# Rotary partner rows: fp32 permutation products on TensorE replaced by SBUF-to-SBUF transfers

## What is computed

```python
def apply_rope(x, cos, sin):           # first stack
    x1, x2 = jnp.split(x, 2, axis=-1)
    return jnp.concatenate([x1 * c - x2 * s, x2 * c + x1 * s], axis=-1)

def rotate(x, ang):                    # second stack, on each half of a head
    x1, x2 = x[..., :m], x[..., m:]
    return jnp.concatenate([x1 * cos - x2 * sin, x2 * cos + x1 * sin], axis=-1)
```

## Time and profile before

| | us |
|---|---|
| median of 3 runs | 2303.76 |
| lowest, highest run | 2297.82, 2307.5 |
| span of the profiled execution | 2301.2 |
| PE busy in it | 2258.3 (98%) |
| DVE busy | 1462.8 (64%) |
| ACT busy | 847.0 (37%) |
| POOL busy | 160.2 (7%) |

### The profile page before, as it was taken

The page is one execution under the profiler, slowest core; times in us unless marked ns, Lnnn a source line. Parts: engine busy times, 40 slices in busy tenths (PEclk is TensorE's granted clock), DMA queues, the critical chain, the costliest instruction groups (busy, mean ns, idle before and its releaser), DMA issues.

```text
span 2301.2 us, 37388 instructions
## 1 busy us (share of the span) xinstructions
PE 2258.3 (98%) x14172; PEld 2033.1 (88%) x14172; DVE 1462.8 (64%) x2310; ACT 847.0 (37%) x1130; POOL 160.2 (7%) x235
## 2 busy tenths in 40 slices
PE   8999999999999999999999999999999999999998
PEld 8999999999999988888888888888888888879998
DVE  4547777556778787678778767773333346556555
ACT  4445444435634432222432222232212234445443
POOL 0110000130000110001001101000000001000000
PEclk9999999999999999999999999999999999999999
DMA  6225665323665565455335545433233223123553
GB/s 230 98 74 195 206 239 174 124 83 103 210 237 187 180 207 183 164 192 177 106 130 204 182 162 199 160 115 110 77 105 109 71 95 127 56 74 128 173 192 128
DMA packets 65483, 343.21 MB, mean 149 GB/s; under 512 B 7152, under 2 KB 10480, under 8 KB 42608
## 3 DMA queue, kind: packets, MB, share of 16 engines
q1 hardware_dynamic: 44656, 266.47, 33.3%
q0 software_dynamic: 20736, 75.51, 9.8%
HBM read 340.90 MB, written 1.05 MB: 149 GB/s over the span
## 4 chain that ended last, share of the span: by engine, by line
PE 79%; issue 11%; DVE 6%; ACT 3%; DMA 1%; POOL 0%; DVEq 0%; SPq 0%; ACTq 0%; POOLq 0%
PE gpt L841 20%; PE gpt L843 19%; PE gpt L842 19%; DVE w_lo L1951 2%; ACT w_hi L1461 2%; PE gpt L938 1%; PE gpt L766 1%; PE gpt L939 1%; PE gpt L940 1%; PE gpt L767 1%; PE gpt L768 1%; PE mbt L1121 1%; PE gpt L1336 1%; PE gpt L1337 1%; PE gpt L1338 1%
## 5 line engine op out<-in xcount | busy, mean ns | idle before, releaser
L841 PE MATMUL gpt<-xn_hi,w_hi 128*128 128x512 f32 (+2 forms) x2256 | 747.3, 331 | 5.7 <-DVE w_lo L1951 5.7
L842 PE MATMUL gpt<-xn_lo,w_hi 128*128 128x512 f32 (+2 forms) x2256 | 742.8, 329 | 0.0
L843 PE MATMUL gpt<-xn_hi,w_lo 128*128 128x512 f32 (+2 forms) x2256 | 742.7, 329 | 0.0
L1951 DVE TENSOR_TENSOR w_lo<-raw,w_hi 128x2048 fp32r<-128x2048 f32 (+2 forms) x280 | 567.6, 2027 | 249.7 <-ACT w_hi L1461 249.5
L1461 ACT ACTIVATE w_hi<-raw 128x2048 fp32r<-128x2048 f32 (+2 forms) x280 | 476.4, 1702 | 390.9 <-PE gpt L843 356.5
L841 PEld LDWEIGHTS gpt<-xn_hi,w_hi 128*128 128x128 f32 x2256 | 426.5, 189 | 46.6 <-issue 7.1
L842 PEld LDWEIGHTS gpt<-xn_lo,w_hi 128*128 128x128 f32 x2256 | 426.6, 189 | 37.6
L843 PEld LDWEIGHTS gpt<-xn_hi,w_lo 128*128 128x128 f32 x2256 | 426.5, 189 | 37.5
L841 PE MATMUL gpt<-mid_hi,w_hi 128*128 128x512 f32 (+2 forms) x996 | 333.1, 334 | 4.7 <-DVE mid_lo L2149 4.5
L842 PE MATMUL gpt<-mid_lo,w_hi 128*128 128x512 f32 (+2 forms) x996 | 332.2, 334 | 0.0
L843 PE MATMUL gpt<-mid_hi,w_lo 128*128 128x512 f32 (+2 forms) x996 | 332.2, 334 | 0.0
(11 more groups left out here) (341 smaller groups left out, 2734.5 us busy)
## 6 DMA issues: line engine op xcount, KB each, us to landing
raw<-in_up_a SPq DMA_DIRECT2D x72, 1024.0 KB, 4.7
ada_w<-in_ada POOLq DMA_DIRECT2D x144, 512.0 KB, 3.5
raw<-in_up_b SPq DMA_DIRECT2D x60, 1024.0 KB, 4.8
raw<-in_down_a SPq DMA_DIRECT2D x48, 768.0 KB, 4.3
raw<-in_down_b SPq DMA_DIRECT2D x48, 640.0 KB, 3.9
raw<-in_win SPq DMA_DIRECT2D x16, 1024.0 KB, 4.8
raw<-in_qkv SPq DMA_DIRECT2D x12, 1024.0 KB, 4.8
raw<-in_wout SPq DMA_DIRECT2D x8, 1024.0 KB, 4.8
```

The costliest lines, as they stand in the source:

```text
L841: mm(o, w_hi[b][:, j, :], hi(k), start=(k == 0), stop=False)
L842: mm(o, w_hi[b][:, j, :], lo(k), start=False, stop=False)
L843: last = mm(o, w_lo[b][:, j, :], hi(k), start=False, stop=(k == kt - 1))
L1951: V.tensor_tensor(w_lo[b][:, 0:tiles, :], raw[b][:, 0:tiles, :], w_hi[b][:, 0:tiles, :].bitcast(F32), ALU.subtract).then_inc(lo_ready, 1)
```

## The change

The three permutation matrices leave `tab`, and the sine table gets the sign: minus in the rows whose partner lies above. The matrix products and their semaphore waits leave PE. In their place the partner rows are copied within SBUF by DMA, two tiles per transfer: for distance d, one DMA for each block of d partitions (2 for d = 64, 4 for 32, 8 for 16). DVE then multiplies the arrived rows by the sine in place, with both operands in SBUF, and adds as before.

```diff
+        def swap_parts(half):
+            return [(a, a ^ half) for a in range(0, P, half)]
 # SP, layer1: between the weight loads
-                for b in range(2):
-                    load(pl + 6, b, dram["rg"][L, 1 + b], MIX_TILES[4 + b])
+                sp.wait_ge(kpe_ready, L + 1)
+                sp.wait_ge(rope_done, L * ROPES1 + 8)
+                for a, c in swap_parts(ROPE // 2):
+                    sp.dma_start(swapped1(8)[a:a + ROPE // 2, :], kpe[c:c + ROPE // 2, :]).then_inc(swap_in[0], 16)
+                load(pl + 6, 0, dram["rg"][L, 1], MIX_TILES[4])
+                sp.wait_ge(qr_gain, L * 2 + 2)
+                sp.wait_ge(rope_done, L * ROPES1 + 9)
+                for a, c in swap_parts(ROPE // 2):
+                    sp.dma_start(ksq[a:a + ROPE // 2, 2:4, :], qf[c:c + ROPE // 2, 4:6, :]).then_inc(swap_in[1], 16)
+                load(pl + 6, 1, dram["rg"][L, 2], MIX_TILES[5])
 # PE: perm, its calls and its waits
-                mm(bank[:, 0:n], tab[:, cp:cp + P], tile, start=True, stop=True).then_inc(perm_ready, 1)
...
 # ACT, layer1
+                def swap(s):
+                    z, m = zq if s < S_RK else zk, 2 * (s % 2)
+                    act.wait_ge(evac_done, done_at(base + s))
+                    if s >= S_RK:
+                        act.wait_ge(rope_done, L * ROPES1 + 2 * (s - S_RK) + 2)
+                    for a, c in swap_parts(P // 2):
+                        nc.scalar.dma_start(ksq[a:a + P // 2, m:m + 2, :], z[c:c + P // 2, m:m + 2, :]).then_inc(swap_in[s % 2], 16)
...
                         copies(s0 + j, [z[:, 2 * j, :], z[:, 2 * j + 1, :]])
+                        if z is not zv:
+                            swap(s0 + j)
 # ACT, differential attention
+            def swap2(i):
+                s = rope2_slot(2 * i)
+                z, m = dq if i < 4 else dk, 2 * (i % 4)
+                act.wait_ge(evac_done, done_at(s))
+                if i >= 4:
+                    act.wait_ge(rope_done, DEPTH * ROPES1 + (4 if i == 4 else 6 if i == 5 else 8 if i == 6 else 10))
+                to = sqb[:, i % 4 if i < 4 else 1 + (i - 4) % 3, :].rearrange("p (h n) -> p h n", n=SEQ)
+                for a, c in swap_parts(16):
+                    nc.scalar.dma_start(to[a:a + 16, :, :], z[c:c + 16, m:m + 2, 0:SEQ]).then_inc(swap2_in[i % 4], 16)
...
                 q_evac(s)
                 split((S_QKV + s) // 2 + 1, s % 2, SIDE_T)
+                swap2(s)
...
             k_evac(0)
+            swap2(4)
             split(k_slot(1) // 2, 0, SIDE_T)
...
                         k_evac((u + 2) // 4)
+                        swap2(4 + (u + 2) // 4)
 # DVE, rope
-                dve.wait_ge(perm_ready, r0 + k + 1)
-                V.tensor_tensor(rb[:, k % 2, :], bank[:, 0:n], tab[:, cs:cs + n], ALU.mult).then_inc(rot_s, 1)
+                arrived(dve)
+                V.tensor_tensor(rb, rb, tab[:, cs:cs + n], ALU.mult).then_inc(rot_s, 1)
```

More of the change, by code:

```diff
@@ L99, in constant_tables @@
     t[64:, C_SEL1] = 1.0
[L101 to L111, removed]
     i = np.arange(P)
@@ L120, in rope @@
         t[:, cc:cc + pos.shape[-1]] = np.cos(ang)
-        t[:, cs:cs + pos.shape[-1]] = np.sin(ang)
+        t[:, cs:cs + pos.shape[-1]] = np.where((i % dim < half)[:, None], -np.sin(ang), np.sin(ang))
     tok = np.arange(T1)[None, :]
@@ L268, in build @@
         kpe_ready = sem("kpe_ready")
-        perm_ready, rot_c, rot_s, rope_done = sem("perm_ready"), sem("rot_c"), sem("rot_s"), sem("rope_done")
+        swap_in, swap2_in = [sem("swap_in0"), sem("swap_in1")], [sem(f"swap2_in{i}") for i in range(4)]
+        rot_c, rot_s, rope_done = sem("rot_c"), sem("rot_s"), sem("rope_done")
         vt_ready, v_ready = sem("vt_ready"), sem("v_ready")
@@ L425, in rope1 @@
             if k < 8:
-                return (zq if k < 4 else zk)[:, k % 4, :], C_PR, C_CR, C_SR
+                return (zq if k < 4 else zk)[:, k % 4, :], C_CR, C_SR
             if k == 8:
-                return kpe[:, :], C_PM, C_CM, C_SM
-            return qf[:, 4 + k - 9, :], C_PM, C_CM, C_SM
+                return kpe[:, :], C_CM, C_SM
+            return qf[:, 4 + k - 9, :], C_CM, C_SM
         def rope2(k):
-            return (dq if k < DHEADS else dk)[:, k % DHEADS, 0:SEQ], C_PD, C_CD, C_SD
+            return (dq if k < DHEADS else dk)[:, k % DHEADS, 0:SEQ], C_CD, C_SD
         DUNITS = [(h, q) for h in range(DHEADS) for q in range(2)]
@@ L450, in rope2_slot, with swapped1, swapped2, wait_swap @@
             return S_QKV + k // 2 if k < DHEADS else k_slot((k - DHEADS) // 2)
-        def rope2_bank(k):
-            return mb[1 + k % 2] if k < DHEADS + 2 else gp[0][k % 2]
+        def swapped1(k):
+            return ksq[:, k % 4 if k < 8 else 3 if k == 10 else 2, :]
+        def swapped2(k):
+            i = k // 2
+            side = sqb[:, i % 4 if i < 4 else 1 + (i - 4) % 3, :]
+            return side[:, (k % 2) * SEQ:(k % 2 + 1) * SEQ]
+        def swap_parts(half):
+            return [(a, a ^ half) for a in range(0, P, half)]
+        SWAPS1 = [2] * 4 + [4, 4]
+        def wait_swap(e, L, k):
+            n = k // 2 if k < 8 else 4 if k == 8 else 5
+            e.wait_ge(swap_in[n % 2], 16 * (L * sum(SWAPS1[n % 2::2]) + sum(SWAPS1[n % 2:n + 1:2])))
+        def wait_swap2(e, k):
+            i = k // 2
+            e.wait_ge(swap2_in[i % 4], 16 * (P // 16) * (i // 4 + 1))
         def wo_bank(m):
@@ L2294, in gated_residual, with rope @@
                 return go
-            def rope(r0, k, item, n, ra, rb, bank):
-                tile, _, _, cs = item
-                dve.wait_ge(perm_ready, r0 + k + 1)
-                V.tensor_tensor(rb[:, k % 2, :], bank[:, 0:n], tab[:, cs:cs + n], ALU.mult).then_inc(rot_s, 1)
+            def rope(r0, k, item, n, ra, rb, arrived):
+                tile, _, cs = item
+                arrived(dve)
+                V.tensor_tensor(rb, rb, tab[:, cs:cs + n], ALU.mult).then_inc(rot_s, 1)
                 dve.wait_ge(rot_s, r0 + k + 1)
                 dve.wait_ge(rot_c, r0 + k + 1)
-                V.tensor_tensor(tile, ra[:, k % 2, :], rb[:, k % 2, :], ALU.add).then_inc(rope_done, 1)
+                V.tensor_tensor(tile, ra[:, k % 2, :], rb, ALU.add).then_inc(rope_done, 1)
             def layer1(L):
@@ L2386, in layer1 @@
                 mix_split(2)
-                rope(L * ROPES1, 8, rope1(8), T1, rot_a, rot_b, ROT2[0])
+                rope(L * ROPES1, 8, rope1(8), T1, rot_a, swapped1(8), lambda e: wait_swap(e, L, 8))
                 q_squares(2)
@@ L2399, in layer1 @@
                 for k in (9, 10):
-                    rope(L * ROPES1, k, rope1(k), T1, rot_a, rot_b, ROT2[k % 2])
+                    rope(L * ROPES1, k, rope1(k), T1, rot_a, swapped1(k), lambda e, k=k: wait_swap(e, L, k))
                 k_squares(2)
@@ L2713, in d_rotations @@
                 for k in ks:
-                    rope(r0, k, rope2(k), SEQ, drot_a, drot_b, rope2_bank(k))
+                    rope(r0, k, rope2(k), SEQ, drot_a, swapped2(k), lambda e, k=k: wait_swap2(e, k))
             dve.wait_ge(xc_ready, ctx_tiles(9))
```

40 lines of the change are left out of this document (7 added, 33 removed).

## The result

The changed kernel takes 2323.0 us (median of 4 runs, 2317.0 to 2324.0) where the kernel before, timed once more beside it, takes 2304.8: a ratio of 1.0081, 95% interval 1.0062 to 1.0100. It is slower by 0.8%, 18 us, where the forecast was 7 us faster, and the time lies outside the range of 2288 to 2310. The profiled execution has a span of 2322.3 us against 2301.2. Timed again in a later session beside the kernel before, the same file gave 2321.1 (2313.1 to 2324.0), ratio 1.0067 (1.0045 to 1.0089).

The account below looks back on a forecast made before the run. The prediction took PE as the bound. Gains of 3.0 us in the two layers, 2.5 ahead of `d_scores(0)` and 1.2 in three units sum to 6.7, taking the median from 2303.8 to 2297.1, range 2288 to 2310.

Parts of the forecast that it names:

- The price of an issue: ACT's DMA issues: 0.39 us from one to the next, 0.34 for the last; two DMAs 0.73, eight 3.07.
- The clock: PE's granted clock: a half-clock stretch of 4 us costs 2; one more or less worth a few us, unassigned.
- I cost them at nothing: Differential attention, issues behind the `dq` copies: no cost, or about 1 us if ACT doesn't issue while it computes.
- What leaves PE: Permutation products removed from both layers and the differential attention: 18.6 us of PE time, if nothing else became late.
- First stack: Each layer: ACT waits for the rope, copies queue behind, PE waits 3.5 us before `k_pe`; 0.2 of 3.7 gained.
- `kpe`: Each layer's `kpe` transfers, issued by SP: last lands at 86.3, DVE wants it at 86.96, so no wait.
- `d_scores(0)`: Start of the differential attention's scores: PE waits 3.5 us for the key rope; gain 2.5 of 6.0 us.
- Units 2, 6, 10: Differential attention: `d_pv` released by `d_at`, gaining 0.4 of 0.86 us each, 1.2 us for three units.
- DVE: DVE's sine product, now reading SBUF twice: as many instructions as before, no cost for product and add together.
- Rival 2: ACT's queue becomes the bound: gain gone at 0.56 us per issue, 2307 to 2308 at 0.62; chance 0.15.
- Rival 1: Issues on ACT cost nearly nothing: gain 14.1 us, time 2289.7; chance 0.20.
- Rival 3: Transfers land late, after 6 us instead of 2.8: 8 us of the gain gone, 2305; chance 0.08.

## Why the prediction was wrong

**The forecast's span was 2294.5; it became 2322.3.** The gap of 27.8 us has three parts; the second and third are estimates.

- **The price of an issue, 11.7 us.** The step that failed is "I choose 0.39, the same kind of queue". The steps measured are 0.64 in the second stack (0.50 in the pairs of the first). From the first issue of a group to ACT's next instruction: in a layer 1.51 and 1.16 where 0.73 stood twice, 2.4 for both layers; 5.95 ahead of the split for `d_scores(0)` and 5.20 in each unit where 3.07 stood, 2.9 + 3 x 2.1. The earlier trace rows held both prices, and the reason given, the same kind of queue, holds for 0.62 as well as for 0.39: it chose nothing, and the upper end was the right one. SP itself shows that the queue was not what decides: it issues the `kpe` transfers in 0.6 each and, 6 us on, a weight load in 0.33:

```profile
83.49 2.50 SPq L528 DMA_DIRECT2D ksq<-kpe  x4
89.63 0.33 SPq L487 DMA_DIRECT2D raw<-in_rg  x1
```

- **The clock, about 12 us** (14 missing, of which 2 passed while PE stood). The prediction called it a term that it couldn't assign, "one more or less is worth a few us either way". But it forecast two new waits of PE of 3.5 us, in three places, and a wait has one sign: with the waits filled the clock never fell at these places. Leaving the term at zero was as large an error as the price.
- **The rest, 4 us.** "I cost them at nothing" was said of the `dq` issues. PE waits 1.4 us for splits and 0.5 for the norm between 1905 and 1970 us, 0.6 before the change: 1.3 us. It is what the prediction gave as the price if ACT couldn't issue beside its own work; it can (a split of 1920.00 runs under issues from 1920.14), and the groups of 5.3 us simply outlast the split. 2.8 us aren't assigned.

**Step by step.** *What leaves PE*, 18.6: right, 17.5 by the kernel without transfers. *First stack*: the mechanism is right (ACT stands for the rope, copies queue behind it, PE waits before `k_pe` in both layers: 3.0, forecast 3.5, and 1.35 and 1.01 before slot 7, forecast none), the start of the gemm is 75.14 instead of 73.9, and the 1.2 between are the issues. *`kpe`*: the last of its transfers is issued at 85.40 and lands 1.9 later, at 87.3 instead of 86.3; DVE comes at 89.52 and doesn't wait, as forecast; for `qf` it waits 0.60, which was not forecast. *`d_scores(0)`*: a wait of 6.2, forecast 3.5. *Units 2, 6, 10*: `d_pv` is released by `d_at`, as forecast, after a wait of 2.5 to 3.0 where the perms had been 0.86. Each unit loses some 1.8 and the clock behind it, instead of gaining 0.4. *DVE*: its sine product takes 0.43 as in the earlier trace rows, and costs nothing.

**The rivals.** Rival 2, ACT's queue as the bound, is what happened, and it had a chance of 0.15. Its own working gave 2307 to 2308 for 0.62 per issue; with some 12 us of clock, which it did not have, this is 2319 to 2320, near the 2321 to 2323 that were measured. Rival 1 had 0.20 for an issue that costs nearly nothing, against rows that all said over 0.3. Rival 3: one of the `zk` transfers near 60 us took 6.5 us to land, and nobody waited for it; landing late had a price only once ACT's queue was out of the way, in the two kernels that issue eight in a row from SP.

**The pages.** The Trainium skill, "DMA: Bandwidth & Descriptors", section "Anatomy of one DMA — SWDGE (gpsimd) path", puts the fixed part of a DMA at about 2.0 us. It says so of DMAs issued from GpSimd, which the prediction left out; for those of ACT and SP the trace agrees at 32 to 68 KB, 2.0, and has 3.8 for the 136 KB of `zk`. (That no run had shown a transfer so small was wrong: the kernel before loads one of 36 KB from HBM at its start, in 4.6.) The Trainium skill's sentence on the same page, in "Issuing engines are not separate DMA queues", that starting a DMA is usually small against the DMA, doesn't hold here: 0.61 of issue for 2.0 of transfer, and eight in a row cost 5.1 for the one that ends last. The Trainium skill's rule on merging disjoint transfers, in "Rules for kernel authors", spoke against this change and came out right, for a cost that its reason, the shared DMA engines, doesn't name: with four DMAs in place of eight 20 us came back. The prediction drew from that page only when a transfer lands, not how many are issued.

## What to carry to other kernels

Price a new DMA in the queue of the engine that issues it, per issue and at the upper end of what the trace shows, and look for what is queued behind the issue and behind its wait; if that engine feeds the bound, move the issue to a queue with nothing behind it before counting any gain. Take work from the engine that is the bound only where its next input is ready: an idle stretch of 3 to 6 us cost itself here and in most cases the clock that fell behind it, so the product that was removed may have been cheap filler. Choose the layout so that a transfer is few DMAs; the order of rows inside a head was free here. An issue that has to stay on a busy engine's queue goes behind the work that others wait for.

## What the runs showed of the hardware

An issue of an SBUF-to-SBUF DMA of 16 or 32 partitions mostly lasts 0.59 to 0.62 us with a step of 0.63 to 0.64, on ACT and on SP, for 32 to 68 KB; two of 64 partitions and 136 KB take 1.12 together, a step of 0.50. SP starts a weight load from HBM, 128 partitions wide, in 0.33. What makes the difference, the source or the number of partitions, no run separates. ACT issues beside its own running activation (1920.14 under 1920.00). The clock did not fall in any filled wait. One stretch isn't explained: in the kernel that only moves `zk`'s issues the clock was 0.60 between 145 and 175 us while PE was busy for 28.85 of the 30,

```profile
145.00:175.00 30.00, 28.85 (x153) 28.61 (x152) 12.06 (x31) 9.44 (x22) 1.01 (x1) 0.60 0.11 36
```

against 0.89 before and 0.94 after the change in the same stretch. Like the one near 104 us, which both profiles of the kernel before have and which lasts from 3 to 17 us in all others but this one, it follows no long wait of PE, and no run here tells what brings it.
